# Scaling the attention probabilities on GpSimd, and splitting the weights in quarter pieces

## The reference

```python
for l in range(DEPTH):                       # 2 layers
    h = rmsnorm(x, attn_norm[l])
    parts = split_columns(h @ w_in[l])       # q, keys, values, gates, GLA and gating inputs
    o_nsa = nsa_mixer(...)                   # below
    x = x + concatenate([o_nsa, o_gla, o_sg]) @ w_out[l]
    h = rmsnorm(x, ffn_norm[l])
    x = x + (silu(h @ w_gate[l]) * (h @ w_up[l])) @ w_down[l]
# nsa_mixer, for 8 heads in 2 groups, per branch (selected, window, compressed):
p = masked_softmax(q @ k.T)                  # rows of 512, causal
o = sum over branches of gate[branch] * (p @ v)
```

## Time and profile before

| | |
|---|---|
| median of 3 runs | 2107.45 us (2106.59 to 2108.77) |
| the profiled execution | 2111.28 us, span 2109.5 us |
| busy PE, weight loads | 1940.0 us (92%), 1502.5 us (71%) |
| busy DVE, ACT, POOL | 1261.9 us (60%), 615.7 us (29%), 1262.8 us (60%) |
| PE waited for DVE's scaling (line 1649) | 24.5 us, 17 times |
| PE waited for `a_lo` (line 1389) | 18.9 us, 8 times |
| POOL waited for PE before `w_hi` | 783.9 us, 259 times |

### The profile page before, as it was taken

How to read it: one execution, slowest core, us unless ns; L and a number is a source line. 1 busy time by engine, 2 the same in 40 slices (tenths; PEclk the granted TensorE clock), 3 DMA queues, 4 the chain that set the end, 5 groups by cost and what they waited for, 6 DMA issues and landing times.

```text
span 2109.5 us, 27159 instructions
## 1 busy us (share of the span) xinstructions
PE 1940.0 (92%) x9830; PEld 1502.5 (71%) x9830; DVE 1261.9 (60%) x1654; ACT 615.7 (29%) x1116; POOL 1262.8 (60%) x560
## 2 busy tenths in 40 slices
PE   6998789999999989988899999996879999989997
PEld 4676557888888766755678888884667777768775
DVE  5866886476266458578575714655946766750353
ACT  4214662210011121266531100113025565550111
POOL 6443017788888754411278978884655555557773
PEclk8999989999999989988999999998999999999998
DMA  5232003343334212300123432542222223312221
GB/s 198 62 96 75 11 11 100 103 143 102 100 126 124 99 60 71 110 21 21 33 84 113 140 98 92 156 118 66 70 65 82 85 80 87 84 60 90 90 90 40
DMA packets 68676, 182.39 MB, mean 86 GB/s; under 512 B 23888, under 2 KB 24144, under 8 KB 68432
## 3 DMA queue, kind: packets, MB, share of 16 engines
q1 hardware_dynamic: 60480, 154.48, 23.7%
q10 hardware_dynamic: 8080, 26.32, 3.9%
HBM read 178.67 MB, written 2.10 MB: 86 GB/s over the span
## 4 chain that ended last, share of the span: by engine, by line
PE 66%; DVE 20%; ACT 8%; issue 4%; DMA 1%; ACTq 0%; DVEq 0%
PE PS L392 20%; PE PS L396 19%; PE PS L395 19%; DVE tmp L1362 2%; DVE xc L1889 2%; DVE a_lo L1389 2%; ACT P L1230 1%; PE PS L681 1%; PE PS L431 1%; PE PS L643 1%; PE PS L631 1%; DVE PS L1599 1%; DVE rg L1950 1%; ACT rg L1301 1%; DVE rg L1944 1%
## 5 line engine op out<-in xcount | busy, mean ns | idle before, releaser
L2052 POOL TENSOR_TENSOR w_hi<-raw,const 128x1024 fp32r<-128x1024 f32 x278 | 559.8, 2014 | 791.2 <-PE PS L392 783.9
L392 PE MATMUL PS<-a_hi,w_hi 128*128 128x512 f32 x1616 | 657.6, 407 | 73.8 <-DVE a_lo L1389 18.9
L2054 POOL TENSOR_TENSOR w_lo<-raw,w_hi 128x1024 fp32r<-128x1024 f32 x278 | 702.9, 2528 | 21.8
L395 PE MATMUL PS<-a_lo,w_hi 128*128 128x512 f32 x1616 | 639.1, 396 | 0.0
L396 PE MATMUL PS<-a_hi,w_lo 128*128 128x512 f32 x1616 | 638.5, 395 | 0.0
L392 PEld LDWEIGHTS PS<-a_hi,w_hi 128*128 128x128 f32 x1616 | 309.2, 191 | 165.1 <-issue 42.2
L396 PEld LDWEIGHTS PS<-a_hi,w_lo 128*128 128x128 f32 x1616 | 309.2, 191 | 67.2
L395 PEld LDWEIGHTS PS<-a_lo,w_hi 128*128 128x128 f32 x1616 | 309.9, 192 | 64.8 <-issue 3.7
L1773 DVE TENSOR_TENSOR work<-PS,rstd 128x512 f32<-128x512 f32 x88 | 60.9, 692 | 150.5 <-PE PS L396 142.2
L392 PE MATMUL PS<-f_hi,w_hi 128*128 128x512 f32 x352 | 138.7, 394 | 0.0
L396 PE MATMUL PS<-f_hi,w_lo 128*128 128x512 f32 x352 | 138.0, 392 | 0.0
(11 more groups left out here) (291 smaller groups left out, 2605.9 us busy)
## 6 DMA issues: line engine op xcount, KB each, us to landing
raw<-weights SPq DMA_DIRECT2D x278, 512.0 KB, 3.5
work<-mod_w ACTq DMA_DIRECT2D x24, 512.0 KB, 3.5
work<-cmp_w ACTq DMA_DIRECT2D x8, 1024.0 KB, 5.4
bias<-rpb SPq DMA_DIRECT2D x256, 12.0 KB
rgw<-rgw ACTq DMA_DIRECT2D x8, 256.0 KB, 2.9
out<-xc SPq DMA_DIRECT2D x8, 256.0 KB, 2.1
const<-const SPq DMA_DIRECT2D x1, 1436.5 KB, 15.1
x<-x_t SPq DMA_DIRECT2D x4, 256.0 KB, 7.0
```

The source lines that it names most:

```text
L392: ins = nc.tensor.matmul(out, wh, hi, start=start, stop=False)
L395: nc.tensor.matmul(out, wh, lo, start=False, stop=False)
L2052: G.tensor_tensor(w_hi[:, r, :, :], raw[:, r, :, :], ones, ALU.mult).then_inc(pool_chain, 1)
L2054: G.tensor_tensor(w_lo[:, r, :, :], raw[:, r, :, :], w_hi[:, r, :, :].bitcast(F32), ALU.subtract)\
```

## The change

Of `scale`, DVE keeps the reciprocal, and `r3` gets two columns for each branch. POOL multiplies each head's row by the reciprocal and by the gate in one instruction with two scalars (new line 2112), so the small product of DVE (1645) and its two long ones (1649) are gone. DVE waits before the reciprocal until POOL has done unit u-2, which used the same columns of `r3`. POOL now has a program that is written out for the loop: the scaling of unit u, then two of the eight parts of a slot's split, where a slot is due (units 1 to 8, 13 to 16, 21 to 24). A part is a quarter of `w_hi` or of `w_lo`.

Outside of the loop a slot is split in four pieces of `w_hi` and four of `w_lo` (each [128, 256]) in the first block's input projections, its output projections and first gate and up slots, and in the second block from its start to the slot of the first gate. From gate 2 of a feed-forward part to its end, and in the second block from the gates on, it stays in one piece.

```diff
+PIECES = 4
...
                 def scale(u):
-                    j, i, br = u // (2 * NT), u // 2 % NT, u % 2
-                    w = (i + 1) * P
-                    both = 2 * j * BR + br
+                    br = u % 2
                     for hh in range(2):
                         dve.wait_ge(*emptying((l, "S", hh, u)))
-                    V.reciprocal(r3[:, 0:2], sums[:, br, 0:2]).then_inc(dve_chain.sem, 1)
-                    dve.wait_ge(dve_chain.sem, dve_chain.raised())
-                    TT(r3[:, 0:2], r3[:, 0:2], gN[:, i, both:both + BR + 1:BR], ALU.mult).then_inc(dve_chain.sem, 1)
-                    dve.wait_ge(dve_chain.sem, dve_chain.raised())
+                    if u >= 2:
+                        dve.wait_ge(scaled.sem, scaled.n - 2)
+                    V.reciprocal(r3[:, 2 * br:2 * br + 2], sums[:, br, 0:2]).then_inc(inverse_ok.sem, 1)
+                    dve.wait_ge(inverse_ok.sem, inverse_ok.raised())
                     for hh in range(2):
-                        pr = work[:, 2 * br + hh, 0:w]
-                        TS(pr, pr, r3[:, hh:hh + 1], None, ALU.mult).then_inc(scaled.sem, 1)
-                        dve.wait_ge(scaled.sem, scaled.raised())
+                        scaled.raised()
...
-            def split(r, arrival, used, chain):
+            def split(r, arrival, used, chain, pieces):
...
-                G.tensor_tensor(w_hi[:, r, :, :], raw[:, r, :, :], ones, ALU.mult).then_inc(pool_chain, 1)
-                pool.wait_ge(pool_chain, chain)
-                G.tensor_tensor(w_lo[:, r, :, :], raw[:, r, :, :], w_hi[:, r, :, :].bitcast(F32), ALU.subtract)\
-                    .then_inc(split_done, 1)
...
+                each = 8 // pieces
+                for n in range(pieces):
+                    k = slice(n * each, (n + 1) * each)
+                    G.tensor_tensor(w_hi[:, r, k, :], raw[:, r, k, :], ones[:, k, :], ALU.mult).then_inc(pool_chain, 1)
+                for n in range(pieces):
+                    k = slice(n * each, (n + 1) * each)
+                    pool.wait_ge(pool_chain, chain + n + 1)
+                    ins = G.tensor_tensor(w_lo[:, r, k, :], raw[:, r, k, :], w_hi[:, r, k, :].bitcast(F32), ALU.subtract)
+                ins.then_inc(split_done, 1)
...
+            def scale(l, u):
+
+                j, i, br = u // (2 * NT), u // 2 % NT, u % 2
+                w = (i + 1) * P
+                both = 2 * j * BR + br
+                pool.wait_ge(inverse_ok.sem, inverse_ok.seen_by("pool"))
+                for hh in range(2):
+                    pr = work[:, 2 * br + hh, 0:w]
+                    gate = gN[:, i, both + BR * hh:both + BR * hh + 1]
+                    G.tensor_scalar(pr, pr, r3[:, 2 * br + hh:2 * br + hh + 1], gate, ALU.mult, ALU.mult)\
+                        .then_inc(scaled.sem, 1)
...
+                for u in range(HEADS * NT):
+                    scale(l, u)
+                    if u in begins:
+                        n, part = begins[u], 0
+                    for _ in range(2):
+                        if part < 2 * PIECES:
+                            split_part(n, part)
+                            part += 1
+                n += 1
+                ahead = PLAN.index(("gate", l, 2))
+                slots(n, ahead, PIECES)
+                n = PLAN.index(("in", l + 1, ORDER[0]) if l + 1 < DEPTH else ("in2", 0))
+                slots(ahead, n, 1)
+            last = PLAN.index(("in2", 6 * KT))
+            slots(n, last, PIECES)
+            slots(last, SLOTS, 1)
```

More of the change, by code:

```diff
@@ new lines, in slots @@
+            def slots(first, last, pieces):
+                n = first
+                while n < last:
+                    turns = (last - n) // RING
+                    if n % RING or not n or turns < 2:
+                        one_slot(n, pieces)
+                        n += 1
+                        continue
+                    begin = n // RING
+                    with pool.Fori(begin, begin + turns) as i:
+                        for r in range(RING):
+                            split(r, i * 16 + 16, i * RING + (r - RING + 1),
+                                  i * (RING * pieces) + (spent[0] + (r - n) * pieces), pieces)
+                    spent[0] += turns * RING * pieces
+                    n += turns * RING
@@ new lines, in _ @@
+            pool.wait_ge(head_in, 16)
+            n = 0
+            for l in range(DEPTH):
+                after = {PLAN.index(("in", l, name)): u for u, (name, step) in BESIDE.items() if not step}
+                fresh = PLAN.index(("in", l, BEFORE[1][0]))
+                after[fresh] = 0
+                begins = {u + 1: slot + RING - 1 for slot, u in after.items()}
+                slots(n, fresh + RING - 1, PIECES)
+                n = fresh + RING - 1
+                part = 2 * PIECES
+                for u in range(HEADS * NT):
[6 more added lines that the diff above has]
+                            part += 1
+                n += 1
+                ahead = PLAN.index(("gate", l, 2))
+                slots(n, ahead, PIECES)
+                n = PLAN.index(("in", l + 1, ORDER[0]) if l + 1 < DEPTH else ("in2", 0))
+                slots(ahead, n, 1)
```

28 lines of the change are left out of this document (19 added, 9 removed).

## The result

The changed kernel takes 2057.16 us at the median of four runs (2055.60 to 2057.67), against 2107.02 for the kernel before on the same chip: a ratio of 0.9762, with a 95% interval of 0.9745 to 0.9779. The forecast was 2065.0. The profiled execution took 2057.22 us.

A forecast was written before the change was run, and what follows sets the result against it. PE, DVE and ACT nearly equally busy in the attention loops, DVE bounding the second block's start; loops -26, second block -12, kernel start -4, output projections -4, pieces' cost +4: -42 us, median 2065, range 2038 to 2104.

The forecast's parts named there:

- Loop, -13 a layer: Attention loops: DVE, freed of scaling, does its extra work while PE and ACT do the unit; -26 us for both layers.
- the product at the loop's start: Attention loop: DVE's small product, held 1.73 us by a split ahead of the loop, is freed by splitting in parts; -1.5 us.
- Rival 4: Attention loop gives nothing: PE and ACT bind it and POOL's longer latency eats what DVE frees; -16, 2091 us; 12 in 100.
- POOL's rate, 0.95 us for 512 columns: Attention loop: POOL's scaling of one head at 512 columns, taken at the rate of `w_hi`, 1.89 us for 1024.
- The chain's terms of +0.39 and -0.2 a unit: Attention loop: wide units lose 0.39 us on the chain through POOL, 16 narrow ones gain 0.2; +3 and -3, together nothing.
- Start of the kernel, -4: Kernel start: DVE takes turns with quarters at 1.15 us instead of whole POOL instructions at 2.5 or so; -4 us (0 to -5).
- Behind the output projection, -2 a layer: Behind the output projection: late sums of squares and PE's 3.0 us wait for `a_lo`; -4 us for both layers (0 to -6).
- Start of the second block, -12: Second block's start: 32 held-up DVE instructions fall from 54.6 to at most 37 us; -12 us, ends -18 and 0.
- the reduction by a third for POOL's own waits: Second block's start: POOL's pieces wait for DVE too, so only two thirds of the 18 us were taken.
- Cost of the pieces, +4: Cut slots: six more POOL instructions cost 0.6 us a slot, showing only where PE takes slots without pause; +4 us (0 to +10).
- Rival 3: Pieces give nothing: their fixed part eats the gain, or POOL keeps its place without a semaphore; -26, 2081 us; 17 in 100.
- Signs of being wrong: A piece over 0.8 us, POOL's scaling past 1.5 us at 512 columns, or PE waiting for `w_lo` in the second block.

The follow-up runs named there:

- e2: The changed kernel with every slot outside the attention loops split in one piece as before; POOL's scaling and the loops' quarters stay: 2101.49 us.
- e6: e4 with each unit's first head scaled on DVE and its second on POOL, both with two scalars in one instruction: 2036.07 us.
- e4: The changed kernel, but a slot's first `w_lo` quarter waits for its last `w_hi` quarter, which leaves a gap once a slot: 2044.91 us.
- e1: The changed kernel with DVE scaling as before and the loops' slots split whole; other cut slots stay in quarters: 2060.70 us.
- e3: The changed kernel with DVE's 8-column product of the gates taking the row mask as a second input, not as a scalar: 2055.44 us.
- e5: The changed kernel with a dead 2-column reciprocal on DVE ahead of the 8-column product of the gates, to move its start: 2054.25 us.
- e9: The changed kernel with a dead two-input product of 512 columns on DVE ahead of the 8-column product of the gates: 2053.35 us.
- e7: e4 with DVE scaling both heads, each in one instruction with two scalars; POOL only splits, in quarters: 2044.30 us.
- e8: e4 with each head's scaling on POOL followed by a second product of the same size, by 1: 2082.35 us.
- e11: e6 with the quartered slots outside the attention loops in eighths; the loops keep quarters: 2059.38 us.
- e12: e6 with quarters also in the feed-forward stages and in the last stage: 2055.03 us.

## Why the prediction was right, and its parts not

- **Loop, -13 a layer: wrong.** The step that failed is "with a third of its work gone DVE can do it while PE and ACT do the unit". DVE's 24.4 us of extra work was not on the path: measured 0 in layer 0 and -7 in layer 1, and some -1.3 a layer where no early stretch of low clock disturbs the comparison. e2 prices the whole term at -7.4 us, not -26. One small part of it came as forecast: the product at the loop's start (182.68, 1.73 us) now takes 0.2, 1.5 us less, and this alone is as large as that gain. Rival 4's half of this, that the loop gives nothing, is what happened in layer 0; its reason, POOL's latency, isn't shown by e6, since halving it gave only 3 us a layer.
- **POOL's rate, 0.95 us for 512 columns: mis-sized to the safe side**, 0.77 measured. The chain's terms of +0.39 and -0.2 a unit, "together nothing", can't be told apart from the result; nothing is what they made.
- **Start of the kernel, -4: right mechanism, -7.5** at the first eviction, beyond my bound of -5. The turns were counted rightly: from 6.4 to 26.4 us the kernel before has eight held-up DVE instructions of 2.0 to 2.7 us, and they now take 0.8 to 1.2. The allowance for the pace of ACT and the loads was too large: behind the first of them DVE waits 1.7 us for ACT, and then goes without a pause to the end of its sums, 7.6 us sooner.
- **Input stages: missing.** No term, and worth more than any other stage but the start of the second block. Layer 1: 224.9 to 211.1 us, -13.8. In this stage PE's waits for DVE had been of a few us each (3.4 at L528, 1.6 at L392, both gone now, with 3.0 more at L528 under "issue"), and I passed over them. PE's busy time fell as well, from 210.2 to 204.2 us, as its mean clock rose from 0.96 to 0.99. These are the two rows, before and after:

```profile
668.80:893.70 224.90, 210.18 (x1240) 161.82 (x1239) 132.36 (x135) 44.74 (x66) 124.18 (x57) 0.96 0.27 87
```

```profile
660.50:871.60 211.10, 204.21 (x1240) 157.69 (x1239) 110.00 (x135) 44.72 (x66) 149.57 (x177) 0.99 0.30 93
```

  Layer 0 would have gained 9 (143.0 to e4's 133.6) and lost 5 instead, because of the 19.29 us.
- **Behind the output projection, -2 a layer: mis-sized**, -4.8 and -5.3, together 10 where my end for both was 6.
- **Start of the second block, -12: mis-sized.** To the last convolution -9.8 and -14.7, so -24.5; of this 6.2 were lost again behind it. Net -18, my lower end. The trace shows where: at the last convolution PE now has 46 matmuls more before it than in the kernel before, two slots' worth, and 11.0 us more to be busy. (In e1, e3, e5 and e9 the last stage, with the same instructions, takes 567.3 to 567.4 us, so about half of the 6.2 comes and goes between executions.)

```profile
1545.10:2109.50 564.40, 525.90 (x2514) 412.22 (x2514) 292.88 (x306) 221.15 (x366) 336.07 (x150) 0.97 0.26 78
```

```profile
1484.80:2055.40 570.60, 536.90 (x2560) 421.03 (x2559) 290.49 (x306) 222.28 (x367) 411.40 (x391) 0.97 0.28 82
```

  DVE's part ends sooner than PE's, and from there on PE sets the time. The 32 DVE instructions take some 32 us for 54.6, better than my bound of 37, and the reduction by a third for POOL's own waits was not called for: PE waits 1.6 us in two waits for `w_lo`.
- **Cost of the pieces, +4: the rate was about right, the +4 itself was not measured apart.** Quarters follow each other at 0.57 and 0.70 us, 0.10 over their share, so a slot costs 0.8 us more for the 0.6 taken. The figure estimated from the Trainium skill (GPSIMD Engine Reference, "3.1 Elementwise — side-by-side cycle accounting"), 0.28 us and a slot of 6 us, is not borne out: a slot takes 5.1. Eighths, at 0.36 and 0.42 us, would make it 0.15.
- **Rival 3 held a part of the truth.** It said that POOL might keep "its place over instructions that follow without a semaphore", and I set it aside because DVE had got in between slots at the start. At 39.02 us it came true, for one instruction, behind quarters that follow without a pause (those of `w_lo` do wait for a semaphore, but it is there already), and cost the 12 us that e4 gives back; elsewhere it didn't.
- **Signs of being wrong.** Two of the three that I named came, though the total was near. A piece was to need under 0.8 us: that holds where DVE is away, but `w_lo`'s quarters outside the loops take 0.86 us in the mean of the whole kernel, and four of them beside the convolution 4.2. And PE does wait for `w_lo` in the second block, 1.6 us. Both limits were set too tight to tell a bad change from a good one. The first `qkv` did come sooner, and the wait of 9.3 us is gone; the loop's 115 us were not reached.
- **Sum.** -42 forecast, -50 measured: the quarters brought 48 for 16, the scaling 7 for 26. The total came out near by errors of opposite sign: as a forecast of this change it was lucky.

## What to carry to other kernels

An engine that is as busy as its neighbours in a loop isn't the bound on that ground: look for who waits at the point that you mean to relieve, and whether another wait of the same length stands right behind it. When a shared resource is held for whole instructions, shorter instructions are worth most where many small waits hold the bounding engine, and cost where the engine that is cut up must keep a rate: count its slot against the consumer's, stage by stage. And keep one wait on its own last result in each slot of the cut-up engine: here that was worth 12 us.

## What the runs showed of the hardware that was not expected

- A DVE product in SBUF stood 19.0 to 19.8 us behind some 30 POOL instructions in a row, in five kernels, in both forms and at both widths; a reciprocal there took 0.17 us. In the seven kernels with a pause of 0.07 us once a slot it took 0.23 to 0.79 us, in four of them (e7, e8, e11, e12) without a pause of POOL while it stood. The Trainium skill (SBUF — State Buffer, "Who interferes with whom") says that whoever issues first has the shared ports for the whole instruction; here the one that came second got them only after a run of instructions. That a single boundary is not always enough, and sometimes is (e7), is what the traces add.
- POOL's product with two scalars per partition: 0.77 us for 512 columns, 0.67 for 384, 0.68 for 256, 0.45 for 128.
- A loop of the same 724 matmuls took 128.7 us at a mean granted clock of 0.96 and 134.5 at 0.89, within one execution; another took 128.7 at 0.92. Where in the loop the lower clock fell made the difference, not its mean.
